# The last stage of a hybrid decoder layer: the gate product on the unnormed, transposed residual

## The reference, cut to what matters

```python
def _rms_norm(x, g):
    xf = x.astype(jnp.float32)
    y = xf * lax.rsqrt(jnp.mean(xf * xf, axis=-1, keepdims=True) + EPS)
    return (y * g.astype(jnp.float32)).astype(x.dtype)
...
    h = h + mixed @ lw['w_out']
    hn = _rms_norm(h, lw['norm_ffn']).reshape(B * L, D_MODEL)
    h = h + _moe(hn, lw['w_router'], lw['b_router'], lw['w_up'], lw['b_up'],
                 lw['w_down'], lw['b_down']).reshape(B, L, D_MODEL)
    gate = jax.nn.sigmoid(_rms_norm(h, lw['norm_ple']) @ lw['w_ple_gate'])
    h = h + gate * (p_l @ lw['w_ple_proj'])
...
y_prompt = _rms_norm(hp, norm_final)
y_sample = _rms_norm(hs, norm_final)
```

## Time and profile before

| | us |
|---|---|
| median of 3 runs | 1230.79 (1230.73 to 1236.77) |
| the profiled execution | 1228.1 |
| its span, first to last instruction | 1226.3 |
| last sum of the experts ends, from the span's start | 1161.4 |
| first matmul of the gate product | 1177.6 |
| last sigmoid of the gate starts | 1210.0 |
| last instruction of DVE ends | 1221.5 |

### The profile page before, as it was taken

How to read it: one execution, slowest core, us unless ns; L and a number is a source line. 1 busy time by engine, 2 the same in 40 slices (tenths; PEclk the granted TensorE clock), 3 DMA queues, 4 the chain that set the end, 5 groups by cost and what they waited for, 6 DMA issues and landing times.

```text
span 1226.3 us, 14536 instructions
## 1 busy us (share of the span) xinstructions
PE 1152.9 (94%) x5741; PEld 494.1 (40%) x5741; DVE 330.3 (27%) x597; ACT 189.8 (15%) x367; POOL 80.2 (7%) x137
## 2 busy tenths in 40 slices
PE   4997898999999999999999999999999999999884
PEld 3664543333333333333333443333333333333364
DVE  5999332121112111111121111112221112112133
ACT  3144321101011010101011111011111011010022
POOL 4664000000000000000000000000000000000000
PEclk9996898999999999999999999999999999999888
DMA  9431524999999999999999999999999999999800
GB/s 297 159 117 61 189 96 185 424 429 428 428 427 429 428 428 428 429 429 429 428 429 429 426 428 427 420 428 427 429 428 429 428 428 428 427 428 427 342 1 35
DMA packets 46428, 438.68 MB, mean 358 GB/s; under 512 B 11056, under 2 KB 15280, under 8 KB 21024
## 3 DMA queue, kind: packets, MB, share of 16 engines
q1 hardware_dynamic: 45760, 437.59, 85.2%
q10 hardware_dynamic: 624, 0.45, 0.1%
HBM read 436.65 MB, written 2.41 MB: 358 GB/s over the span
## 4 chain that ended last, share of the span: by engine, by line
PE 67%; DMA 23%; DVE 6%; ACT 2%; issue 1%; ACTq 0%; DVEq 0%; SPq 0%
PE ps L1068 27%; DMA ring_up<-in_w_up_dram 23%; PE ps L1086 12%; PE ps L1040 4%; PE ps L1004 4%; PE ps L1292 2%; PE ps L785 2%; PE ps L1058 2%; PE ps L586 1%; PE ps L1206 1%; PE ps L1050 1%; PE ps L1075 1%; DVE ps L1749 1%; PE ps L641 1%; PE ps L920 1%
## 5 line engine op out<-in xcount | busy, mean ns | idle before, releaser
L1068 PE MATMUL ps<-ring_up,region 128*64 128x512 f32 x2048 | 451.1, 596 | 10.1 <-DMA ring_up<-in_w_up_dram 10.1
L1068 PEld LDWEIGHTS ps<-ring_up,region 128*64 128x64 f32 x2048 | 143.7, 137 | 293.2 <-issue 271.6
L1086 PE MATMUL ps<-ring_dn,region 128*64 128x512 f32 x1024 | 229.0, 599 | 0.4 <-ACT region L1557 0.4
L2081 DVE TENSOR_SCALAR region<-ps 128x512 f32<-128x512 f32 (+1 forms) x33 | 22.6, 684 | 459.0 <-PE ps L1068 445.4
L1086 PEld LDWEIGHTS ps<-ring_dn,region 128*64 128x64 f32 x1024 | 70.8, 137 | 132.6 <-issue 128.3
L2075 DVE TENSOR_TENSOR fb<-fb,ps 128x528 f32<-128x528 f32 x64 | 45.0, 704 | 253.7 <-PE ps L1004 244.7
L1040 PE MATMUL ps<-n_tok,region 128*64 128x512 f32 (+1 forms) x384 | 94.1, 608 | 1.3 <-DVE region L2024 1.3
L1553 ACT ACTIVATE region<-region 128x512 f32<-128x512 f32 x32 | 20.2, 630 | 454.6 <-DVE region L2081 454.6
L1567 ACT ACTIVATE region<-ps 64x512 f32<-64x512 f32 x64 | 37.9, 592 | 246.1 <-PE ps L1086 245.7
L1004 PE MATMUL ps<-region 128*128 128x264 f32 x256 | 74.5, 413 | 0.9 <-DVE fb L2075 0.9
L547 POOL COPY region<-kst 128x64 f32 (+1 forms) x33 | 7.8, 237 | 984.6 <-PE ps L1068 948.2
(11 more groups left out here) (382 smaller groups left out, 820.8 us busy)
## 6 DMA issues: line engine op xcount, KB each, us to landing
ring_up<-in_w_up_dram SPq DMA_DIRECT2D x132, 2048.0 KB, 20.5
ring_dn<-in_w_down_dram SPq DMA_DIRECT2D x66, 2048.0 KB, 18.3
ring_up<-in_w_in_dram SPq DMA_DIRECT2D x4, 1024.0 KB, 10.2
ring_dn<-in_w_out_dram SPq DMA_DIRECT2D x1, 4096.0 KB
ring_up<-in_w_ple_gate_dram SPq DMA_DIRECT2D x4, 1024.0 KB, 20.6
x_tok<-in_x_prompt_dram SPq DMA_DIRECT2D x2, 512.0 KB
ring_up<-in_w_in_dram SPq DMA_DIRECT2D x2, 512.0 KB, 8.7
ring_up<-in_w_glu_dram SPq DMA_DIRECT2D x1, 1024.0 KB
```

Source lines behind the costliest of these rows:

```text
L1068: m = mm(ps[64 * (q % 2):64 * (q % 2) + 64, HID_B + q // 2, :], xe[:, k % 4, k // 4], ring_up[:, k, q * 512:(q + 1) * 512], start=False, s ...
L1086: m = mm(ps[64 * half:64 * half + 64, OUT_B, :], act_t[:, f % 4, 64 * (f // 4):64 * (f // 4) + 64], ring_dn[:, f, 512 * half:512 * half + ...
L2081: V.tensor_scalar(gl, bank(HID_B, n_), LIMIT, None, ALU.min).then_inc(Z["g_rdy"], 1)
```

## The change

- The first pair's outputs are added to `fb` instead of copied, so `fb` ends up as residual plus experts, transposed. `x_tok` is no longer touched in the tail.
- The gate product runs on this `fb` as it is. The norm's weights (`V_PLE` columns of `vecs`) are multiplied into `w_gate` in place, blocks 0 to 3 by POOL behind the first two loads, blocks 4 to 7 by ACT behind the last two.
- The root comes from the squares of `fb` on ACT (`h_square`, which lies in `n_tok`), summed over features by eight matmuls with a matrix of ones into bank 2, root on ACT, inverse on DVE (`h_rstd`, 264 wide). DVE multiplies each gate block by it on the way out of PSUM (`gz_lin`), ahead of the sigmoid.
- DVE adds `fb` to the gated embedding in `fa`. PE turns each block back two rounds later (`turn_back`) into banks 4 to 7, 2 and 3 (`Y_B`), where the whole result stays. ACT squares it there in halves, DVE makes the last product from there.
- The tables for root and sigmoid are asked for by an instruction on one element ahead of their use. Each chunk's store waits for its own chunk.

```diff
-MOE_T = (0, 6, 4)
+Y_B, SSQ_B = (4, 6, 2), 2
...
+        h_square = n_flat[:, 0:KD * T].rearrange("p (k t) -> p k t", k=KD)
+        h_rstd = g_lim[:, 0:T]
...
                 sp.wait_ge(Z["up_free"], (n + (NE - 1)) * UP + (k + 1))
                 sp.dma_start(w_gate[:, 2 * k:2 * k + 2], A["w_ple_gate"][0].rearrange("(s k p) n -> s p k n", p=P, k=2)[k]
-                             ).then_inc(ld_gate_w, 16)
+                             ).then_inc(ld_gate[k // 2], 16)
+            for c in range(2):
+                sp.wait_ge(Z["f_out"], c + 1)
+                sp.dma_start(O[0][0, c * P:(c + 1) * P, :], n_tok[:, c]).then_inc(Z["st_y"], 16)
             sp.wait_ge(Z["f_out"], 3)
-            for c in range(2):
-                sp.dma_start(O[0][0, c * P:(c + 1) * P, :], n_tok[:, c]).then_inc(Z["st_y"], 16)
             sp.dma_start(O[1].rearrange("b l d -> (b l) d"), n_tok[0:NB, 2]).then_inc(Z["st_y"], 16)
...
+            pool.wait_ge(ld_gate[0], 32)
+            for b in range(4):
+                nc.gpsimd.tensor_scalar(w_gate[:, b], w_gate[:, b], vecs[:, V_PLE + b:V_PLE + b + 1], 1.0,
+                                        ALU.mult, ALU.mult).then_inc(Z["wg_rdy"], 1)
...
-            pe.wait_ge(Z["cmb_read"], (n_visits + PAIRS) * 4)
-            for c, (t0, nt) in enumerate(CHUNKS):
+            def turn_back(o):
+
+                pe.wait_ge(Z["gz_mul"], o + 1)
+                for c, (t0, nt) in enumerate(CHUNKS):
+                    m = tr(ps[0:nt, Y_B[c] + o // 4, (o % 4) * P:(o % 4 + 1) * P], fa[:, o, t0:t0 + nt], ident)
+                if o % 4 == 3:
+                    m.then_inc(Z["back_ps"], 1)
+
+            for o in range(KD):
+                if o >= 2:
+                    pe.wait_ge(Z["gz_lin"], o - 1)
                 for k in range(KD):
-                    m = tr(ps[0:nt, MOE_T[c] + k // 4, (k % 4) * P:(k % 4 + 1) * P], fb[:, k, t0:t0 + nt], ident)
-                m.then_inc(Z["back_ps"], 1)
-
-            for c, (t0, nt) in enumerate(CHUNKS):
-                pe.wait_ge(Z["norm_scaled"], 6 + c + 1)
-                for half in range(2):
-                    b_ = (0, 1, 6, 7, 2, 5)[2 * c + half]
-                    for k in range(4):
-                        m = tr(ps[:, b_, k * nt:(k + 1) * nt],
-                               n_tok[0:nt, c, (4 * half + k) * P:(4 * half + k + 1) * P], ident[0:nt, 0:nt])
-                    m.then_inc(Z["norm_ps"], 1)
-            pe.wait_ge(Z["norm_sb"], 17)
-            pe.wait_ge(ld_gate_w, 64)
-
-            def back(half):
-
-                pe.wait_ge(Z["gz_mul"], 4 * (half + 1))
-                for c, (t0, nt) in enumerate(CHUNKS):
-                    n_ = 3 * half + c
-                    if n_ >= 2:
-                        pe.wait_ge(Z["back_add"], 12 + n_ - 1)
-                    for k in range(4):
-                        m = tr(ps[0:nt, 4 + n_ % 2, k * P:(k + 1) * P], fa[:, 4 * half + k, t0:t0 + nt], ident)
+                    if o == 0 and k % 2 == 0:
+                        pe.wait_ge(Z["cmb_read"], (n_visits + PAIRS) * 4 + (k // 2 - 3))
+                    if o == 0 and k == 0:
+                        pe.wait_ge(Z["wg_rdy"], KD)
+                    m = mm(bank(o % 2, T), w_gate[:, k, o * P:(o + 1) * P], fb[:, k, :], start=(k == 0), stop=(k == KD - 1))
+                m.then_inc(Z["gz_ps"], 1)
+                if o == 0:
+                    for k in range(KD):
+                        if k % 2 == 0:
+                            pe.wait_ge(Z["norm_ssq"], 6 + k // 2 + 1)
+                        m = mm(bank(SSQ_B, T), ones, h_square[:, k, :], start=(k == 0), stop=(k == KD - 1))
                     m.then_inc(Z["back_ps"], 1)
-
-            for o in range(KD):
-                b_ = o % 4
-                if o >= 4:
-                    pe.wait_ge(Z["gz_sig"], o - 3)
-                for k in range(KD):
-                    m = mm(bank(b_, T), w_gate[:, k, o * P:(o + 1) * P], fb[:, k, :], start=(k == 0), stop=(k == KD - 1))
-                m.then_inc(Z["gz_ps"], 1)
-                if o == 5:
-                    back(0)
-            back(1)
+                if o >= 2:
+                    turn_back(o - 2)
+            turn_back(KD - 2)
+            turn_back(KD - 1)
...
-            further_visits(act, visit)
-
+            n_visits = further_visits(act, visit)
+
+            act.wait_ge(ld_gate[1], 32)
+            for b in range(4, KD):
+                f(w_gate[:, b], w_gate[:, b], ACT.Copy, scale=vecs[:, V_PLE + b:V_PLE + b + 1]).then_inc(Z["wg_rdy"], 1)
+            for j in range(4):
+                act.wait_ge(Z["cmb_read"], (n_visits + PAIRS) * 4 + (j - 3))
+                f(h_square[:, 2 * j:2 * j + 2], fb[:, 2 * j:2 * j + 2], ACT.Square).then_inc(Z["norm_ssq"], 1)
+            f(small[0:1, 103:104], eps[0:1], ACT.Sqrt)
+            act.wait_ge(Z["back_ps"], 2)
+            f(h_rstd, bank(SSQ_B, T), ACT.Sqrt, scale=1.0 / D, bias=eps).then_inc(Z["norm_root"], 1)
+            f(small[0:1, 101:102], eps[0:1], ACT.Sigmoid)
+
+            def y_squares(c, half):
+
+                nt = CHUNKS[c][1]
+                return f(n_tok[0:nt, c, 512 * half:512 * half + 512], ps[0:nt, Y_B[c] + half, :], ACT.Square,
+                         accum_out=stat[0:nt, c, 3 * half:3 * half + 1])
+
+            for o in range(KD):
+                act.wait_ge(Z["gz_lin"], o + 1)
+                f(sg_t[:, o % 2], sg_t[:, o % 2], ACT.Sigmoid).then_inc(Z["gz_sig"], 1)
+                if o == 6:
+                    act.wait_ge(Z["back_ps"], 3)
+                    for c in range(3):
+                        y_squares(c, 0).then_inc(Z["norm_ssq"], 1)
+            f(small[0:1, 102:103], eps[0:1], ACT.Sqrt)
+            act.wait_ge(Z["rstd"], 6)
+            act.wait_ge(Z["back_ps"], 4)
             for c, (t0, nt) in enumerate(CHUNKS):
-                act.wait_ge(Z["back_add"], 9 + c + 1)
-                f(n_tok[0:nt, c], x_tok[0:nt, c], ACT.Square, accum_out=stat[0:nt, c, 0:1]).then_inc(Z["norm_ssq"], 1)
-            roots(2)
-            for o in range(KD):
-                act.wait_ge(Z["gz_ps"], o + 1)
-                if o >= 2:
-                    act.wait_ge(Z["gz_mul"], o - 1)
-                f(sg_t[:, o % 2], bank(o % 4, T), ACT.Sigmoid).then_inc(Z["gz_sig"], 1)
-            for c, (t0, nt) in enumerate(CHUNKS):
-                act.wait_ge(Z["back_add"], 12 + 4 + c)
-                f(n_tok[0:nt, c], x_tok[0:nt, c], ACT.Square, accum_out=stat[0:nt, c, 0:1]).then_inc(Z["norm_ssq"], 1)
-            roots(3)
...
                     acc, out = fb[:, 2 * j:2 * j + 2], ps[:, b_:b_ + 2, 0:T]
-                    if isinstance(n_, int) and n_ == 0:
-                        V.tensor_copy(acc, out).then_inc(Z["cmb_read"], 1)
-                    else:
+                    if not isinstance(n_, int) or n_ > 0:
                         dve.wait_ge(Z["cmb_read"], 4 * n_ + j - 3)
-                        V.tensor_tensor(acc, acc, out, ALU.add).then_inc(Z["cmb_read"], 1)
+                    V.tensor_tensor(acc, acc, out, ALU.add).then_inc(Z["cmb_read"], 1)
 
             def activation(t, n_=512):
 
@@ -2170,39 +2185,25 @@
             added(PAIRS - 1, last=True)
             further_visits(dve, visit, expert_of=True)
 
-            for c, (t0, nt) in enumerate(CHUNKS):
-                dve.wait_ge(Z["back_ps"], 1 + c + 1)
-                xh = x_tok[0:nt, c].rearrange("p (a n) -> p a n", a=2)
-                V.tensor_tensor(xh, xh, ps[0:nt, MOE_T[c]:MOE_T[c] + 2, :], ALU.add).then_inc(Z["back_add"], 1)
-
-            norm_rows(2)
-            for c, (t0, nt) in enumerate(CHUNKS):
-                for half in range(2):
-                    dve.wait_ge(Z["norm_ps"], 11 + 2 * c + half + 1)
-                    b_ = (0, 1, 6, 7, 2, 5)[2 * c + half]
-                    V.tensor_tensor(fb[:, 4 * half:4 * half + 4, t0:t0 + nt],
-                                    ps[:, b_, 0:4 * nt].rearrange("p (k n) -> p k n", k=4),
-                                    col(vecs[:, V_PLE + 4 * half:V_PLE + 4 * half + 4], nt), ALU.mult
-                                    ).then_inc(Z["norm_sb"], 1)
-
-            def residual(half):
-                for c, (t0, nt) in enumerate(CHUNKS):
-                    n_ = 3 * half + c
-                    dve.wait_ge(Z["back_ps"], 4 + n_ + 1)
-                    xh = x_tok[0:nt, c, 512 * half:512 * half + 512]
-                    V.tensor_tensor(xh, xh, ps[0:nt, 4 + n_ % 2, :], ALU.add).then_inc(Z["back_add"], 1)
-
+            dve.wait_ge(Z["norm_root"], 7)
+            chain(V.reciprocal(h_rstd, h_rstd))
             dve.wait_ge(Z["pp_sb"], KD)
             for o in range(KD):
+                dve.wait_ge(Z["gz_ps"], o + 1)
+                V.tensor_tensor(sg_t[:, o % 2], bank(o % 2, T), h_rstd, ALU.mult).then_inc(Z["gz_lin"], 1)
                 dve.wait_ge(Z["gz_sig"], o + 1)
-                V.tensor_tensor(fa[:, o, :], fa[:, o, :], sg_t[:, o % 2], ALU.mult).then_inc(Z["gz_mul"], 1)
-                if o == 5:
```

(14 more changed lines are left out.)

12 lines of the change are left out of this document (8 added, 4 removed).

## The result

| | before | changed |
|---|---|---|
| median, us | 1231.13 (4 runs, 1230.73 to 1236.77) | 1214.87 (4 runs, 1213.80 to 1219.48) |
| ratio to before | 1 | 0.9865, 95% interval 0.9826 to 0.9903 |
| profiled execution, span, us | 1226.3 | 1212.0 |

The kernel is faster by 1.35%, 16.3 us between the medians; between the two profiled executions the spans differ by 14.3. The forecast was 1217.2 with 1212.5 to 1224.

A forecast was written before the change was run, and what follows sets the result against it. The tail's 64.9 us bound it: short dependent steps around PE's gate product. Start -11.4, product +3.9, end -6.1 make -13.6 us, so 1230.8 becomes 1217.2, range 1212.5 to 1224.

The forecast's parts named there:

- low clock costs in group 0: First matmul group of the gate product: 4.1 us at half clock cost 2.05 us, bounded by 1.5 and 3.9.
- The start: Gate product's first matmul, set by ACT's scaling of the weights: at 1166.2 against 1177.62, 11.4 us earlier.
- a last expert that ends at another time than 1161: Ahead of the tail: the change should leave the experts' end alone, so another time would show the prediction wrong.
- The product: Nine matmul groups on PE with low clock and transposes: stretch grows from 32.4 to 36.3 us.
- The reciprocal: DVE's inverse of the root over 264 elements: 1.8 us, hidden under group 1, so PE doesn't wait.
- The end: Residual, norm and stores behind the product: shrinks from 16.3 to 10.2 us.
- The low end: Range's lower limit, 1212.5: faster clock rise, fast store, better overlap of squares and roots, profiled execution's time as base.
- 1 (POOL): Weight scaling: POOL at 3.0 us each sets the product's start at 1168.1; time 1219.1, chance 0.11.
- 2 (a dearer switch of tables): Final root: another 1.4 us beyond the table load, end 1.3 later; time 1218.5, chance 0.08.
- 3: Product and stores: late clock rise (+1.9), dear reciprocal (PE waits 1.5), slow stores (+1.1); 1221.7, chance 0.07.
- 4: Product rounds: PE waits 0.7 us in each of eight for turned-back columns, halving the gain; 1223, chance 0.08.
- 5: Weight scaling: POOL's in-place work delays PE, over 0.5% slower from 7.4 us each; priced at 1240, chance 0.03.

The follow-up runs named there:

- e3: Changed kernel, but POOL goes three times over its four gate weight blocks; median 1218.93 us, ratio 0.9911.
- e4: Changed kernel with a semaphore for each gate weight load and scaling spread (ACT three blocks, POOL five); median 1212.71 us, ratio 0.9862.
- e1: Changed kernel, but the three stores again wait for all three chunks; median 1215.55 us, ratio 0.9890.
- e2: Changed kernel without the one-element instruction that asks early for the root's table; median 1218.78 us, ratio 0.9900.
- e6: Kernel before with only the change's end: root's table asked for early, each store waiting for its own chunk; median 1225.20 us, ratio 0.9968.
- e8: Changed kernel with scaling spread behind each load, squares summed on DVE, and transposes moved behind the last group; median 1210.03 us, ratio 0.9849.
- e9: e8 plus six unneeded matmuls behind the experts' last, ahead of PE's jump; median 1207.82 us, ratio 0.9839.

## Why the prediction was right

| step | predicted | measured |
|---|---|---|
| ACT's four scalings end | 1166.1 | 1165.84 |
| POOL's four end | 1163.8 | 1161.1 |
| product starts | 1166.2 | 1165.98 |
| low clock costs in group 0 | 2.05 | 2.2 |
| one set of transposes | 0.39 | 0.33 |
| reciprocal over 264 | 1.8 | 1.80 |
| DVE reads group 7 | 1202.5 | 1201.93 |
| last transposes end, ACT has its table | 1204.9, 1204.9 | 1204.37, 1204.33 |
| DVE's last end | 1210.3 | 1209.80 |
| from there to the span's end | 2.4 | 2.2 |
| span | 1212.7 | 1212.0 |

**The start** was the largest term (11.4 predicted, 11.6 measured) and e3 and e4 show from both sides that the scaling sets it. One thing could have gone wrong and did not count: in this execution the clock was low during the last expert's products until 1156.3 (before, until 1153.3), and the experts' last sum ended at 1162.7, 1.3 later than before. The landing of the weights and ACT's scaling covered that. In the kernel before, where PE's turning waits for that sum, it would have gone into the time. The prediction had named a last expert that ends at another time than 1161 as a sign of being wrong. It appeared, and the start held, because it had come to hang on the landing.

**The product** grew from 32.4 to 36.0 (36.3 predicted). The rise of the clock was seen here:

```profile
1163.00:1164.00 1.00, 0.00 (x0) 0.00 (x0) 0.00 (x0) 1.00 (x2) 0.00 (x0) 0.58 0.03 8
...
1169.00:1170.00 1.00, 1.00 (x3) 0.76 (x3) 0.00 (x0) 0.47 (x2) 0.00 (x0) 0.50 0.00 0
1170.00:1171.00 1.00, 1.00 (x6) 0.83 (x5) 0.00 (x0) 0.00 (x0) 0.00 (x0) 1.00 0.00 0
```

The granted clock fell while PE had nothing to do, stayed at 1.2 GHz until 1170, and rose 4.0 us after PE had begun. That the prediction took 4.1 and met 4.0 is in part luck: with the same code the group took 5.6 to 6.4 in six profiles, and 6.9 in e3, so the range given for that term was needed. Two smaller terms were off. The 0.26 from the last matmul to its reader was 0.03: in the kernel before group 0 itself took 5.27, so 0.2 of that belonged to the low clock, which here too cost 0.2 more than half its length. And the five sets of transposes took 1.65, not 2.0.

**The reciprocal** hid as forecast. The row that it was scaled from, the difference of two widths and not the whole of one, gave its size to a hundredth.

**The end** shrank from 16.3 to 10.1 (10.2 predicted), with the terms near their sizes: e1 gives 2.5 for the stores (2.4 predicted), e2 1.3 for the load. The steps of DVE were 1.38 apart and not 1.47, as its reciprocal is partly overlapped with the product ahead of it.

**The term that was off** is POOL. I doubled the row of 512 elements, 0.93, and got 1.9 for 1024; it took 1.12. In that row's time DVE was at work on `n_tok` beside POOL, so the faster row wasn't an undisturbed one either; no run separates what DVE and what a fixed part of each instruction had in it. The outcome doesn't change, since ACT sets the start, but the rival that rested on it (1 in 9) was over-weighted: POOL was done 4.8 us before ACT. The sentence of the Trainium skill on shared interfaces ("GPSIMD Engine Reference", Key points) agrees with the rows: in e4 one such instruction took 1.12 from 1160.50 on, with DVE adding out of PSUM beside it until 1161.47.

**The median** fell by 16.3, more than the 13.6 forecast. The spans differ by 14.3 of it. The rest is the base: I carried over the 2.7 by which the median of before lay above its profiled execution. By the four runs here it is 3.0 (1231.13 to 1228.1), and the changed kernel's median lies 1.1 above its own execution (1213.8), which was the fastest of its four. That is chance and no mechanism. The low end was also added up wrongly: its four parts give 1212.9 and not 1212.5.

**The rivals.** 1 (POOL) and 2 (a dearer switch of tables) are refuted by the trace and e2. Of 3, the clock can rise later (group 0 up to 6.9), but not 7.9 us in, and the reciprocal isn't dear. 4 isn't seen: between 1165.98 and 1201.9 PE has no idle time. 5 is real as a mechanism (e3) and was far from its threshold.

## What to carry to other kernels

Where a stage is a string of short steps that wait for each other, look for what commutes: a norm's root can be applied to the product's results instead of its inputs, and its weights to the product's weights while these wait for nothing else. What then sets the start is the last operand's landing and whatever is done to it after, so spread that work over all idle engines and give each load its own semaphore. Ask for the activation table and issue each store as soon as each can go; here that was worth 3.8 us in the kernel before (e6), and 2.5 and 1.4 in the changed one (e1, e2). And count from an event near the change when what lies ahead varies more than what is measured.

## What was not expected of the hardware

- POOL's multiplication of 128x1024 fp32 in place took 1.12 us with DVE idle or reading PSUM, 1.09 ns for each element, where rows of before have 1.8 to 2.9 ns for each element, at half the width and with DVE at work on SBUF. Which of the two makes the difference isn't shown.
- PE idled 2.1 to 2.9 us behind the experts, where its program has a jump (before, e4, e8), and not at all in e9, where matmuls were still queued.
- The clock after a start from rest: group 0 with 3.6 us of work took 5.6 to 6.9 us in nine profiles of the changed kernel and its variants, and 3.6 where 4.2 us of other matmuls ran directly ahead of it.
